# The router reads the residual through weights scaled by the modulation, and ACT modulates all channels there

## The chip, the cores and the metric

One core of one Trainium2 chip runs the whole program. The metric is device time in microseconds of one execution; the program before was executed three times for its median. TensorE (PE) multiplies, DVE and ACT work elementwise, SP issues the weight loads; POOL (GpSimd) does almost nothing.

## The reference, cut to what matters

Two layers (Hyena, then RG-LRU) are each followed by a mixture of 16 experts with a router that both share. 384 tokens (128 context, 256 latent) of width 1024 pass through. The part that the change touches is the norm, the modulation and the router before each expert layer:

```python
h = rms_norm(x, norm_moe[i]) * (1 + sc2) + sh2         # sc2, sh2 per stream: context or latent
scores = softmax(h @ router_w)                          # 16 experts
sel = scores + router_bias
best_group = argmax(sum of the top 2 of sel in each group of 4)
idx = top 2 of sel within best_group;  gates = scores[idx] / sum(scores[idx])
x = x + g2 * sum_j gates_j * ((silu(h @ w1[e_j]) * (h @ w3[e_j])) @ w2[e_j])
```

With r the reciprocal root of a token, h @ W = r * (x @ (norm_moe * (1 + sc2) * W)) + sh2 @ W. The program after the change computes the logits in this second form; h itself is still needed, by the experts.

## The kernel before, in words

Activations lie channel by channel: `xc` (the residual) and `hT` hold 8 channel tiles of 128 partitions by 384 tokens. Instructions of each engine are written out in order by hand, one function per engine (`_(sp)`, `_(act)`, `_(pe)`, `_(dve)`), and are tied by counting semaphores (`S("name")`); `before(name, index)` gives how many counts earlier layers or norms have made, from the table `PER`. A norm has a tag: 0 and 2 are those of the mixers, 1 and 3 those of the expert layers.

From the residual to the experts, for tags 1 and 3, the order is this. DVE adds each output tile to `xc` (L1760); ACT squares it (L559); TensorE sums the squares with a matrix of ones, in four column tiles of 32 (`norm_sums`); ACT takes the root (L571), DVE the reciprocal (L1440), TensorE spreads it over all partitions (`norm_spread`, products of `rs` with a column of the identity). DVE multiplies `xc` by it, channel by channel (L1447). Then `modulate` applies scale and shift: ACT to the first BY_ACT = 5 channels (two instructions each, one for each stream, L580), DVE to the last 3 (L1456). The router multiplies `rw` (16 experts padded to 32 columns) with `hT`: two accumulation steps in each of four column tiles, so that PSUM has four partial sums. ACT copies them (L810), TensorE transposes them, DVE adds the four parts (L1776), takes the maximum and subtracts it, ACT takes the exponential (L813) and DVE selects group and experts in some 27 small linked instructions up to the mask (L1819). TensorE counts with the mask each token's rank in its expert's queue; DVE makes one-hot matrices (`pick`, L1862) of the ranks. TensorE meanwhile transposes `hT` into token order, six tiles of four transposes (`token_tile`), which ACT evicts into `h` (L805). The first expert gathers its tokens as `h` times `pick` (the products PS<-stack,h).

`spin(n)` is n products whose result nobody reads. In `norm` one stands before and two behind the spread; in the router five stand behind the token tiles and three behind the ranks.

Every weight goes through ten slots of 2 MB, loaded by SP. At the residual's end four loads of the first two experts are released; the next waits for the route and the first expert's first product. A matmul of fp32 appears as two records in the trace.

Of the kernel before, what the change touches and what calls it, by code (L numbers as in the profile page):

```python
# [12 lines left out]
ALU = mybir.AluOpType  # L13
# [3 lines left out]
P = 128  # L17
D = 1024
KD = D // P
# [17 lines left out]
_COLS = [("ident", P), ("earlier_rows", P // 2), ("all_rows", P // 2), ("ones", 32), ("iota_base", BASE), ("iota_extra", EXTRA), ("limits", NX), ("desc", NE)]  # L37
# [36 lines left out]
def constants():  # L74
# [13 lines left out]
    put("iota_extra", np.tile(np.arange(EXTRA), (P, 1)))  # L88
    put("desc", np.tile(NE - np.arange(NE), (P, 1)))
# [35 lines left out]
class Chain:  # L125
# [5 lines left out]
    def link(self, instruction):  # L131
# [6 lines left out]
PER = dict(sq=8, ss_mm=1, rms=1, rinv=1, rb_mm=1, nrm=8, hT_act=BY_ACT, hT_dve=KD - BY_ACT, ada_mm=12, o_mm=8, x_upd=8,  # L138
           rt_mm=3, rt_ev=1, rt_exp=1, rt_max=1, rt_mask=1, tok_mm=6, tok=6, route=1, pick=18, gpick=16,
           xT_mm=16, xT=16, w1_mm=16, w13_mm=16, sig=16, hid=16, gpT_mm=8, gpT=8, hidT_mm=16, hidT=16, w2_mm=16, yo=16,  # L140
           c_mm=64, acc_done=64)
def before(name, index):

    return PER[name] * index

# [109 lines left out]
def program(nc, A, y_prompt, y_sample, new_state):  # L255
    where, (pool, pool_order, pool_count) = plan(), pool_plan()
    with ExitStack() as ctx:
# [91 lines left out]
        chosen = misc[:, 1728:1760].bitcast(BF16)  # L349
        earlier_rows, all_rows = const("earlier_rows").bitcast(BF16), const("all_rows").bitcast(BF16)  # L350
# [175 lines left out]
        def _(act):  # L526
# [46 lines left out]
            def modulate(tag):  # L573
# [3 lines left out]
                for k in range(BY_ACT):  # L577
# [10 lines left out]
            def norm(tag, sem, value):  # L588
# [4 lines left out]
                modulate(tag)  # L593
# [79 lines left out]
            def mixer0():  # L673
# [8 lines left out]
                modulate(0)  # L682
# [109 lines left out]
            for l in range(LAYERS):  # L792
# [9 lines left out]
                def token_tile(i):  # L802
                    act.wait_ge(S("tok_mm"), before("tok_mm", l) + i + 1)
# [3 lines left out]

                table(ACT.Exp)
                act.wait_ge(S("rt_mm"), before("rt_mm", l) + 1)
                a.activation(pre[:, 0, :], PS[:, 0, 0:N], ACT.Copy).then_inc(S("rt_ev"), 1)  # L810
                token_tile(0)
                act.wait_ge(S("rt_max"), before("rt_max", l) + 1)
                a.activation(rt(0), rt(0), ACT.Exp).then_inc(S("rt_exp"), 1)  # L813
                for i in range(1, 6):
                    token_tile(i)
# [28 lines left out]
        def _(pe):  # L844
# [136 lines left out]
            def channel_ready(tag, k):  # L981

                if k < BY_ACT:
                    pe.wait_ge(S("hT_act"), before("hT_act", tag) + k + 1)
                else:
                    pe.wait_ge(S("hT_dve"), before("hT_dve", tag) + k - BY_ACT + 1)

            def norm_ready(tag):
                pe.wait_ge(S("hT_act"), before("hT_act", tag + 1))
                pe.wait_ge(S("hT_dve"), before("hT_dve", tag + 1))  # L990

            def norm(tag):
                norm_sums(tag)
                if tag == 1:
                    pe.wait_ge(S("v_in"), 16)
                spin(1, bank=3)
# [1044 lines left out]
```

## Time and profile before

| | |
|---|---|
| three executions | 1561.53, 1564.23, 1564.71 us; median 1564.23 |
| the profiled execution | 1562.67 us, its span 1560.9 us |
| granted TensorE clock, mean | 0.993 |
| PE busy | 1499.3 us (96%) |
| DVE busy | 633.1 us (41%) |
| ACT busy | 297.5 us (19%) |
| DMA | 495.31 MB, mean 317 GB/s |

The span runs from the first to the last instruction; the execution's own time has the launch around it. Busy PE includes fillers, so 96% doesn't say that TensorE bounds all stages: what ends a stage is read from the chain of waits.

### The profile page before, as it was taken

The page shows a single profiled execution, that of the slowest core. Times are in us where ns is not written, and L with a number is a line of the kernel's source. Part 1 is how long each engine was busy: PE and PEld are TensorE (multiplying, and loading weights), DVE is VectorE, ACT ScalarE, POOL GpSimd, SP SyncE. Part 2 cuts the span into 40 slices and gives each one's busy share as a digit, 9 for nine tenths or more (in the row PEclk, how much of TensorE's full clock was granted, in tenths as well). Part 3 has the DMA queues.
Part 4 walks back from the last instruction along what each step waited for, and adds up shares of the span by engine and source line. Part 5 has one row for each costly group of instructions (what it writes and reads, how often), then busy time and mean ns, then how long its engine had stood idle before and what let it go on. Part 6 is the DMA issues. An engine that isn't in the chain of part 4 may idle for free.

```text
span 1560.9 us, 21439 instructions
## 1 busy us (share of the span) xinstructions
PE 1499.3 (96%) x7870; PEld 718.6 (46%) x7871; DVE 633.1 (41%) x1846; ACT 297.5 (19%) x503; POOL 0.2 (0%) x4
## 2 busy tenths in 40 slices
PE   9999999999899999999999899999999999999986
PEld 4454555654444344344353455555344434344433
DVE  4445665434324322322333548735132332432333
ACT  4422222121010011011010357623011001011001
POOL 0000000000000000000000000000000000000000
PEclk9999999999999999999999999999999999999999
DMA  9548667762969999999996701525899999999992
GB/s 345 186 138 304 252 253 266 290 278 113 418 278 396 426 427 427 426 426 427 427 423 240 254 1 54 215 109 216 365 423 425 427 426 422 425 427 426 425 393 95
DMA packets 67712, 495.31 MB, mean 317 GB/s; under 512 B 4608, under 2 KB 21264, under 8 KB 28368
## 3 DMA queue, kind: packets, MB, share of 16 engines
q1 hardware_dynamic: 66048, 489.33, 76.7%
q10 hardware_dynamic: 1616, 5.33, 1.0%
q8 instruction: 32, 0.52, 0.1%
q14 instruction: 16, 0.13, 0.0%
HBM read 493.06 MB, written 1.58 MB: 317 GB/s over the span
## 4 chain that ended last, share of the span: by engine, by line
PE 78%; DMA 11%; DVE 5%; ACT 3%; issue 1%; DVEq 0%; SPq 0%; ACTq 0%
PE PS L846 76%; DMA halves<-in_moe_w 11%; PE PS L850 2%; DVE xc L1872 1%; ACT hT L580 1%; DVE misc L1690 0%; DVE halves L1690 0%; DVE halves L1683 0%; DVE halves L1681 0%; ACT hT L829 0%; DVE halves L1509 0%; DVE halves L1682 0%; ACT halves L640 0%; ACT halves L742 0%; ACT h L641 0%
## 5 line engine op out<-in xcount | busy, mean ns | idle before, releaser
L846 PE MATMUL PS<-halves,hT 128*64 128x512 f32 x3072 | 670.1, 595 | 16.1 <-DMA halves<-in_moe_w 13.9
L846 PEld LDWEIGHTS PS<-halves,hT 128*64 128x64 f32 x3072 | 217.8, 137 | 450.1 <-issue 426.9
L846 PE MATMUL PS<-hT,halves 128*128 128x384 f32 x640 | 214.9, 490 | 0.1
L846 PE MATMUL PS<-halves 128*32 128x512 f32 (+5 forms) x928 | 194.1, 510 | 1.8 <-ACT halves L543 0.7
L846 PEld LDWEIGHTS PS<-hT,halves 128*128 128x128 f32 x640 | 119.3, 190 | 98.0 <-issue 18.2
L1953 DVE COPY misc<-PS 64x512 f32<-64x512 f32 x32 | 21.9, 683 | 320.9 <-PE PS L846 320.9
L846 PEld LDWEIGHTS PS<-halves 128*128 128x128 f32 (+2 forms) x928 | 96.6, 158 | 85.3 <-issue 44.4
L1872 DVE SCALAR_TENSOR_TENSOR xc<-PS,MOD,xc 128x128 f32<-128x128 f32 x336 | 112.4, 410 | 13.8 <-PE PS L846 11.8
L602 ACT ACTIVATE hT<-PS 128x512 f32<-128x512 f32 x32 | 19.1, 598 | 430.5 <-PE PS L846 430.5
L846 PE MATMUL PS<-stack,h 128*128 128x128 f32 x768 | 93.5, 279 | 5.4 <-issue 4.3
L846 PEld LDWEIGHTS PS<-stack,h 128*128 128x128 f32 x768 | 89.5, 194 | 18.1 <-issue 16.5
L1941 DVE TENSOR_TENSOR hT<-hT,PS 128x512 f32<-128x512 f32 x32 | 22.0, 688 | 152.1 <-PE PS L846 152.1
L617 ACT ACTIVATE hT<-PS 128x512 f32<-128x512 f32 x32 | 19.1, 597 | 310.8 <-PE PS L850 310.8
L1936 DVE TENSOR_TENSOR hT<-hT,PS 128x512 f32<-128x512 f32 x32 | 22.0, 687 | 103.4 <-ACT hT L602 103.4
L846 PE MATMUL PS<-hT,misc 128*128 128x384 f32 x128 | 53.1, 500 | 4.8 <-DVE RG L1953 3.3
L846 PE MATMUL PS<-hT,RG 128*128 128x384 f32 x128 | 51.3, 486 | 0.0
L1474 DVE SCALAR_TENSOR_TENSOR h<-pre,VT,h 128x127 f32<-128x127 f32 (+1 forms) x80 | 29.6, 412 | 43.9 <-ACT h L658 28.6
L654 ACT ACTIVATE pre<-PS,VT 128x384 f32<-128x384 f32 x24 | 14.0, 581 | 160.5 <-PE PS L846 160.5
L846 PE MATMUL PS<-h,halves 128*128 128x384 f32 x128 | 42.6, 486 | 0.0
L850 PE MATMUL PS<-cst,hT 128*128 128x128 f32 x224 | 35.0, 284 | 4.2 <-DVE xc L1872 3.3
L846 PE MATMUL PS<-halves,misc 128*32 128x256 f32 x640 | 35.6, 380 | 2.4 <-ACT misc L607 2.4
L850 PEld LDWEIGHTS PS<-cst,hT 128*128 128x128 f32 x224 | 30.5, 178 | 12.2 <-DVE xc L1872 4.4
(239 smaller groups left out, 1025.2 us busy)
## 6 DMA issues: line engine op xcount, KB each, us to landing
halves<-in_moe_w SPq DMA_DIRECT2D x192, 2048.0 KB, 17.8
halves<-in_ada_w SPq DMA_DIRECT2D x48, 1024.0 KB, 6.5
halves<-in_hy_w_in SPq DMA_DIRECT2D x12, 1024.0 KB, 5.2
halves<-in_rg_w_in SPq DMA_DIRECT2D x4, 2048.0 KB, 19.1
halves<-in_hy_w_out SPq DMA_DIRECT2D x4, 1024.0 KB, 9.4
halves<-in_rg_w_out SPq DMA_DIRECT2D x2, 2048.0 KB, 10.6
halves<-in_rg_wa SPq DMA_DIRECT2D x1, 2048.0 KB, 8.4
halves<-in_rg_wx SPq DMA_DIRECT2D x1, 2048.0 KB, 12.4
```

Source lines behind the costliest of these rows:

```text
L580: ins = a.activation(hT3[:, k, cs], hT3[:, k, cs], ACT.Identity, bias=MOD[:, l, 8 * sh + k, s:s + 1], scale=MODA[:, tag, k, s:s + 1])
L602: a.activation(hid, PS[:, 2, :], ACT.Sigmoid).then_inc(S("sig"), 1)
L617: a.activation(hidT, PS[:, 2, :].rearrange("p (c m) -> p c m", m=P), ACT.Copy) \
L654: a.activation(pre[:, ct % 2, :], PS[:, ct % 2, 0:N], ACT.Identity, bias=VT[:, 0, HB + ct:HB + ct + 1]).then_inc(S("in_ev0"), 1)
L846: return nc.tensor.matmul(out, lhsT, rhs, start=start, stop=stop)
L850: return nc.tensor.transpose(out, in_, ident[0:n, 0:n])
L1474: last = v.scalar_tensor_tensor(o, i, weight, o, ALU.mult, ALU.add)
L1872: ins = v.scalar_tensor_tensor(xc[:, k, cs], PS[:, bank, cs], MOD[:, l, 8 * G2 + k, s:s + 1], xc[:, k, cs], ALU.mult, ALU.add)
L1936: ch.link(v.tensor_tensor(hid, hid, PS[:, 2, :], ALU.mult))
L1941: v.tensor_tensor(hid, hid, PS[:, 3, :], ALU.mult).then_inc(S("hid"), 1)
L1953: last = v.tensor_copy(yo[g][BASE * r:BASE * r + BASE, :], PS[BASE * g:BASE * g + BASE, 6, :])
```

## The change

The names are those of the kernel. `by_act(tag)`, `turned_act` and `turned_dve` replace the fixed split: at odd tags all eight channels are ACT's. DVE scales the router's weights for both streams ahead of the residual's updates (`rw_mod`). TensorE multiplies the shift with the plain weights (two columns, one for each stream) and the residual with the scaled ones (`router_raw`), between the sums and the spread. ACT copies both results. DVE multiplies the copied logits by the reciprocal root, before it applies the norm to channels 0 to 5; `fold` is a constant of four stacked identities, with which TensorE adds the four partial sums, transposes, and adds the shift's part in one product pair per token tile. DVE takes maximum and difference from PSUM, then applies the norm to channels 6 and 7. ACT modulates channels 0 to 3, takes the exponential, modulates 4 to 7 and only then evicts the token tiles, in the order 0, 2, 4, 1, 3, 5. The fillers of the odd norms go; two stand behind the router's products, one behind the token tiles, three behind the ranks as before.

```diff
@@ -34,7 +34,7 @@
 NX = (N - BASE) // EXTRA
 
 
-_COLS = [("ident", P), ("earlier_rows", P // 2), ("all_rows", P // 2), ("ones", 32), ("iota_base", BASE), ("iota_extra", EXTRA), ("limits", NX), ("desc", NE)]
+_COLS = [("ident", P), ("earlier_rows", P // 2), ("all_rows", P // 2), ("ones", 32), ("iota_base", BASE), ("iota_extra", EXTRA), ("limits", NX), ("desc", NE), ("fold", NE)]
 _HYENA_COLS = [("fwd_lat", 2 * LAT), ("fwd_ctx", CTX), ("inv_lat", 4 * LAT // 2), ("inv_ctx", CTX)]
 COL, NCOL = {}, 0
 for _name, _n in _COLS + _HYENA_COLS:
@@ -86,6 +86,7 @@
     put("ones", np.ones((P, 32)))
     put("iota_base", np.tile(np.arange(BASE), (P, 1)))
     put("iota_extra", np.tile(np.arange(EXTRA), (P, 1)))
+    put("fold", np.tile(np.eye(32)[:, 0:NE], (4, 1)))
     put("desc", np.tile(NE - np.arange(NE), (P, 1)))
     put("limits", np.tile(BASE + EXTRA * np.arange(NX), (P, 1)))
     lag = []
@@ -135,13 +136,28 @@
 
 
 
-PER = dict(sq=8, ss_mm=1, rms=1, rinv=1, rb_mm=1, nrm=8, hT_act=BY_ACT, hT_dve=KD - BY_ACT, ada_mm=12, o_mm=8, x_upd=8,
-           rt_mm=3, rt_ev=1, rt_exp=1, rt_max=1, rt_mask=1, tok_mm=6, tok=6, route=1, pick=18, gpick=16,
+PER = dict(sq=8, ss_mm=1, rms=1, rinv=1, rb_mm=1, nrm=8, bias_mm=1, bias_ev=1, raw_mm=1, rw_mod=1, ada_mm=12, o_mm=8, x_upd=8,
+           rt_mm=2, rt_ev=1, rt_exp=1, rt_max=1, rt_mask=1, tok_mm=6, tok=6, route=1, pick=18, gpick=16,
            xT_mm=16, xT=16, w1_mm=16, w13_mm=16, sig=16, hid=16, gpT_mm=8, gpT=8, hidT_mm=16, hidT=16, w2_mm=16, yo=16,
            c_mm=64, acc_done=64)
 def before(name, index):
 
     return PER[name] * index
+
+
+def by_act(tag):
+
+    return KD if tag % 2 else BY_ACT
+
+
+def turned_act(tag):
+
+    return sum(by_act(u) for u in range(tag))
+
+
+def turned_dve(tag):
+
+    return KD * tag - turned_act(tag)
 
 
 
@@ -570,11 +588,11 @@
                 act.wait_ge(S("ss_mm"), tag + 1)
                 a.activation(rs, PS[:, NORM_BANK[tag], 0:96], ACT.Sqrt, bias=eps, scale=1.0 / D).then_inc(S("rms"), 1)
 
-            def modulate(tag):
+            def modulate(tag, ks):
                 l = tag // 2
                 sh = SH2 if tag % 2 else SH1
                 act.wait_ge(S("modA"), tag + 1)
-                for k in range(BY_ACT):
+                for k in ks:
                     act.wait_ge(S("nrm"), before("nrm", tag) + k + 1)
                     for s, cs in streams:
                         ins = a.activation(hT3[:, k, cs], hT3[:, k, cs], ACT.Identity,
@@ -590,7 +608,8 @@
                     table(ACT.Sqrt)
                 squares(tag, NORM_ORDER[tag], sem, value)
                 norm_root(tag)
-                modulate(tag)
+                if tag % 2 == 0:
+                    modulate(tag, range(BY_ACT))
 
             def expert_layer(l):
                 with act.Fori(0, NE // UNROLL) as group:
@@ -799,20 +818,24 @@
 
                 norm(2 * l + 1, "x_upd", 8 * l + 1)
 
-                def token_tile(i):
-                    act.wait_ge(S("tok_mm"), before("tok_mm", l) + i + 1)
+                def token_tile(n):
+                    i = TOKEN_ORDER[n]
+                    act.wait_ge(S("tok_mm"), before("tok_mm", l) + n + 1)
 
                     a.activation(h[:, i // 2, i % 2 * HALF:i % 2 * HALF + HALF].rearrange("p (k c) -> p k c", k=4),
                                  PS[:, 2 + i, :].rearrange("p (c k) -> p k c", k=4), ACT.Copy).then_inc(S("tok"), 1)
 
+                act.wait_ge(S("bias_mm"), l + 1)
+                a.activation(bias_col, PS[:, 4, 0:2], ACT.Copy).then_inc(S("bias_ev"), 1)
+                act.wait_ge(S("raw_mm"), l + 1)
+                a.activation(pre[:, 0, :], PS[:, 5, 0:N], ACT.Copy).then_inc(S("raw_ev"), 1)
                 table(ACT.Exp)
-                act.wait_ge(S("rt_mm"), before("rt_mm", l) + 1)
-                a.activation(pre[:, 0, :], PS[:, 0, 0:N], ACT.Copy).then_inc(S("rt_ev"), 1)
-                token_tile(0)
+                modulate(2 * l + 1, range(4))
                 act.wait_ge(S("rt_max"), before("rt_max", l) + 1)
                 a.activation(rt(0), rt(0), ACT.Exp).then_inc(S("rt_exp"), 1)
-                for i in range(1, 6):
-                    token_tile(i)
+                modulate(2 * l + 1, range(4, KD))
+                for n in range(6):
+                    token_tile(n)
                 for i, bank in enumerate(TOKEN_BANKS):
                     act.wait_ge(S("xT_mm"), before("xT_mm", l) + i + 1)
                     a.activation(xT[:, i, :, :], PS[:, bank, :].rearrange("p (c m) -> p c m", m=P), ACT.Copy) \
@@ -981,21 +1004,23 @@
             def channel_ready(tag, k):
 
                 if k < BY_ACT:
-                    pe.wait_ge(S("hT_act"), before("hT_act", tag) + k + 1)
+                    pe.wait_ge(S("hT_act"), turned_act(tag) + k + 1)
                 else:
-                    pe.wait_ge(S("hT_dve"), before("hT_dve", tag) + k - BY_ACT + 1)
+                    pe.wait_ge(S("hT_dve"), turned_dve(tag) + k - BY_ACT + 1)
 
             def norm_ready(tag):
-                pe.wait_ge(S("hT_act"), before("hT_act", tag + 1))
-                pe.wait_ge(S("hT_dve"), before("hT_dve", tag + 1))
+                pe.wait_ge(S("hT_act"), turned_act(tag + 1))
+                pe.wait_ge(S("hT_dve"), turned_dve(tag + 1))
 
             def norm(tag):
                 norm_sums(tag)
-                if tag == 1:
-                    pe.wait_ge(S("v_in"), 16)
-                spin(1, bank=3)
-                norm_spread(tag)
-                spin(2, bank=3)
+                if tag % 2:
+                    router_raw(tag // 2)
+                    norm_spread(tag)
+                else:
+                    spin(1, bank=3)
+                    norm_spread(tag)
+                    spin(2, bank=3)
 
             def in_tile(ct):
                 w = piece(("in", ct // 2)).rearrange("p (k n) -> p k n", k=8)
@@ -1141,22 +1166,39 @@
                     last = tr(PS[:, 2 + i, P * c:P * c + P], hT3[:, 4 * half + c, P * t:P * t + P])
                 last.then_inc(S("tok_mm"), 1)
 
-            def router(l):
-                pe.wait_ge(S("rw_in"), 16)
+            def router_raw(l):
+                pe.wait_ge(S("rw_mod"), l + 1)
                 for kk in range(2):
                     for j in range(4):
-                        channel_ready(2 * l + 1, j + 4 * kk)
-                        last = mm(PS[32 * j:32 * j + 32, 0, 0:N], rw[:, j + 4 * kk, :], hT3[:, j + 4 * kk, :],
+                        last = mm(PS[32 * j:32 * j + 32, 4, 0:2], rw[:, j + 4 * kk, :], MOD[:, l, 8 * SH2 + j + 4 * kk, :],
                                   kk == 0, kk == 1)
-                last.then_inc(S("rt_mm"), 1)
-                token_tile(l, 0)
+                last.then_inc(S("bias_mm"), 1)
+                for s, cs in streams:
+                    for kk in range(2):
+                        for j in range(4):
+                            last = mm(PS[32 * j:32 * j + 32, 5, cs], rw_mod[:, s, j + 4 * kk, :], xc[:, j + 4 * kk, cs],
+                                      kk == 0, kk == 1)
+                last.then_inc(S("raw_mm"), 1)
+
+            def router(l):
+                pe.wait_ge(S("bias_ev"), l + 1)
                 pe.wait_ge(S("rt_ev"), before("rt_ev", l) + 1)
                 for t in range(NT):
-                    last = tr(PS[:, 1, P * t:P * t + P], pre[:, 0, P * t:P * t + P])
+                    s = 0 if t == 0 else 1
+                    out = PS[:, 6, NE * t:NE * t + NE]
+                    mm(out, bias_col[:, s:s + 1].broadcast_to([P, P]), const("fold"), True, False)
+                    last = mm(out, pre[:, 0, P * t:P * t + P], const("fold"), False, True)
                 last.then_inc(S("rt_mm"), 1)
-                for i in range(1, 6):
+                if l == 0:
+                    pe.wait_ge(S("v_in"), 16)
+                spin(2)
+                for n, i in enumerate(TOKEN_ORDER):
+                    if n in (0, 3):
+                        pe.wait_ge(S("hT_act"), turned_act(2 * l + 1) + 4 * (i % 2) + 4)
+                    if 2 + i == 6:
+                        pe.wait_ge(S("rt_max"), before("rt_max", l) + 1)
                     token_tile(l, i)
-                spin(5)
+                spin(1)
                 pe.wait_ge(S("rt_mask"), before("rt_mask", l) + 1)
                 mask = e3(chosen[:, 0:3 * NE])
                 mm(PS[:, 1, 0:4 * NE], earlier_rows, chosen, True, False)
@@ -1439,16 +1481,15 @@
                 dve.wait_ge(S("rms"), tag + 1)
                 v.reciprocal(rs, rs).then_inc(S("rinv"), 1)
 
-            def norm_apply(tag):
+            def norm_apply(tag, ks):
                 if tag % 2 == 0 and tag:
                     dve.wait_ge(S("acc_done"), ADDED + before("acc_done", tag // 2))
                 dve.wait_ge(S("rb_mm"), tag + 1)
-                for k in range(KD):
+                for k in ks:
                     v.tensor_tensor(hT3[:, k, :], xc[:, k, :], PS[:, 1, 0:N], ALU.mult).then_inc(S("nrm"), 1)
 
             def modulate(tag):
-                l = tag // 2
-                sh = SH2 if tag % 2 else SH1
+                l, sh = tag // 2, SH1
                 dve.wait_ge(S("modA"), tag + 1)
                 for k in range(BY_ACT, KD):
                     dve.wait_ge(S("nrm"), before("nrm", tag) + k + 1)
@@ -1754,6 +1795,12 @@
                     for s, cs in streams:
                         ins = v.tensor_scalar(xc[:, dc, cs], xc[:, dc, cs], gb[:, dc, s:s + 1], None, ALU.add)
                 link(ins)
+                dve.wait_ge(S("modA"), 2 * l + 2)
+                dve.wait_ge(S("rw_in"), 16)
+                for s in range(2):
+                    ins = v.tensor_tensor(rw_mod[:, s, :, :], rw[:, :, :],
+                                          MODA[:, 2 * l + 1, :, s:s + 1].broadcast_to([P, KD, 32]), ALU.mult)
+                ins.then_inc(S("rw_mod"), 1)
                 for dc in range(KD):
                     dve.wait_ge(S("o_mm"), 8 * l + dc + 1)
                     for s, cs in streams:
@@ -1770,12 +1817,18 @@
                 def wide(ap, n=NE):
                     return ap.unsqueeze(2).broadcast_to([P, NT, n])
 
-                link(v.memset(chosen[:, 3 * NE:], 0.0))
-                dve.wait_ge(S("rt_mm"), before("rt_mm", l) + 2)
-                parts = PS[:, 1, 0:N].rearrange("p (t j e) -> p t e j", t=NT, j=4)[:, :, 0:NE, :]
-                link(v.tensor_reduce(L, parts, AX, ALU.add))
-                link(v.tensor_reduce(mx, L, AX, ALU.max))
-                v.tensor_tensor(L, L, wide(mx), ALU.subtract).then_inc(S("rt_max"), 1)
+                tag = 2 * l + 1
+                v.memset(chosen[:, 3 * NE:], 0.0)
+                norm_inverse(tag)
+                dve.wait_ge(S("raw_ev"), l + 1)
+                dve.wait_ge(S("rb_mm"), tag + 1)
+                v.tensor_tensor(pre[:, 0, :], pre[:, 0, :], PS[:, 1, 0:N], ALU.mult).then_inc(S("rt_ev"), 1)
+                norm_apply(tag, range(6))
+                dve.wait_ge(S("rt_mm"), before("rt_mm", l) + 1)
+                logits = PS[:, 6, 0:NT * NE].rearrange("p (t e) -> p t e", t=NT)
+                link(v.tensor_reduce(mx, logits, AX, ALU.max))
+                v.tensor_tensor(L, logits, wide(mx), ALU.subtract).then_inc(S("rt_max"), 1)
+                norm_apply(tag, range(6, KD))
                 dve.wait_ge(S("rt_exp"), before("rt_exp", l) + 1)
                 link(v.tensor_reduce(sm, L, AX, ALU.add))
                 link(v.reciprocal(sm, sm))
@@ -1826,7 +1879,7 @@
                 link(v.tensor_reduce(sm, scores, AX, ALU.add))
                 link(v.reciprocal(sm, sm))
                 link(v.tensor_tensor(gates[:, :, 0:NE], scores, wide(sm), ALU.mult))
-                dve.wait_ge(S("rt_mm"), before("rt_mm", l) + 3)
+                dve.wait_ge(S("rt_mm"), before("rt_mm", l) + 2)
                 ranks = PS[:, 1, 0:NT * NE].rearrange("p (t e) -> p t e", t=NT)
                 link(v.scalar_tensor_tensor(eq, ranks, 1.0, mask, ALU.add, ALU.mult))
                 link(v.tensor_scalar(rankm[:, :, 0:NE], eq, -1.0, None, ALU.add))
@@ -1962,7 +2015,6 @@
                     norm(2 * l)
                     mixer1()
                 residual(l)
-                norm(2 * l + 1)
                 route(l)
                 expert_layer(l)
 
@@ -1990,6 +2042,7 @@
 SPREAD_BANKS = (6, 4, 5, 7, 1, 0, 3, 4)
 
 TOKEN_BANKS = (0, 5)
+TOKEN_ORDER = (0, 2, 4, 1, 3, 5)
 X_COMBINE = ((0, 0), (2, 2), (4, 6), (6, 4), (1, 5), (3, 7), (5, 3), (7, 1))
 
 _INS = ["ada_w", "norm_final", "hy_w_in", "hy_f_w3", "hy_w_out", "rg_w_in", "rg_wa", "rg_wx", "rg_w_out", "moe_w1",
```

## Rows read from the trace of the kernel before

**Rows 1.** page part 4, the chain's shares by engine

```profile
PE 78%; DMA 11%; DVE 5%; ACT 3%; issue 1%; DVEq 0%; SPq 0%; ACTq 0%
```

**Rows 2.** chain of waits in order of time, layer 0: start, us, what

```profile
342.57 1.15 PE PS L846 x8
...
344.39 4.49 ACT hT L580 x10
348.89 1.28 ACT L586
350.82 0.56 PE PS L850 x3
361.24 1.08 DVE stack L1862 x6
...
621.42 23.30 DMA halves<-in_moe_w
```

**Rows 3.** timeline of DVE, layer 0: start, us, instruction, count, idle

```profile
321.53 0.74 DVE L1760 SCALAR_TENSOR_TENSOR xc<-PS,MOD,xc 128x128 f32<-128x128 f32 x2 [15.68 <-PE PS L846]
...
343.74 3.81 DVE L1447 TENSOR_TENSOR hT<-xc,PS 128x384 f32<-128x384 f32 x8 [1.22 <-PE PS L846]
...
352.98 0.20 DVE L1780 TENSOR_REDUCE misc<-misc 128x3 f32<-128x48 f32 x1 [0.31 <-ACT misc L813]
...
358.87 0.21 DVE L1819 TENSOR_TENSOR misc<-misc 128x48 bf16<-128x48 f32 x1
...
360.41 0.21 DVE L1831 SCALAR_TENSOR_TENSOR misc<-PS,misc 128x48 f32<-128x48 f32 x1
```

**Rows 4.** timeline of ACT, layer 0

```profile
350.19 0.20 ACT L586 ACTIVATE small<-small 128x1 f32<-128x1 f32 x1
...
352.70 0.24 ACT L813 ACTIVATE misc<-misc 128x48 f32<-128x48 f32 x1 [1.31 <-DVE misc L1778]
352.85 2.53 ACT L805 ACTIVATE h<-PS 128x512 f32<-128x512 f32 x5
```

**Rows 5.** timeline of TensorE, layer 0

```profile
351.21 2.35 PE L850 MATMUL PS<-cst,hT 128*128 128x128 f32 x20
353.39 4.46 PE L846 MATMUL PS<-VT,cst 128*128 128x512 f32 x10
359.14 0.26 PE L846 MATMUL PS<-misc,cst 128*128 128x64 bf16 x4 [1.29 <-DVE misc L1819]
```

**Rows 6.** busy us by window: PE, PEld, DVE, ACT, POOL; clock, DMA share, GB/s

```profile
362.00:384.00 22.00, 21.08 (x138) 10.82 (x137) 6.97 (x33) 3.07 (x4) 0.00 (x0) 1.00 0.00 1
```

**Rows 7.** chain of waits, layer 1

```profile
1063.99 1.15 PE PS L846 x8
...
1065.81 4.49 ACT hT L580 x10
```

**Rows 8.** timeline of DVE, layer 1

```profile
1045.47 0.74 DVE L1760 SCALAR_TENSOR_TENSOR xc<-PS,MOD,xc 128x128 f32<-128x128 f32 x2 [3.44 <-PE PS L846]
...
1074.04 0.20 DVE L1780 TENSOR_REDUCE misc<-misc 128x3 f32<-128x48 f32 x1 [0.31 <-ACT misc L813]
```

**Rows 9.** timeline of TensorE, 14 to 42 us

```profile
32.13 2.79 PE L846 MATMUL PS<-cst,halves 128*128 128x32 f32 x24
```

**Rows 10.** timeline of TensorE, 340.7 to 344 us

```profile
340.51 0.74 PE L846 MATMUL PS<-h,cst 128*32 128x96 f32 x12
```

**Rows 11.** groups by form, 318 to 420 us: busy, mean ns | idle before

```profile
L846 PE MATMUL PS<-halves,misc 128*32 128x256 f32 x128 | 7.1, 380 | 0.5 <-ACT misc L607 0.5
...
L846 PE MATMUL PS<-h,cst 128*32 128x96 f32 x64 | 1.7, 249 | 0.1
...
L1896 DVE TENSOR_TENSOR misc<-misc,PS 128x256 f32<-128x256 f32 x1 | 0.4, 422 | 2.6 <-PE PS L846 2.6
```

**Rows 12.** busy time by window, layer 1, with the granted clock

```profile
1100.00:1106.00 6.00, 3.55 (x16) 1.04 (x13) 0.69 (x1) 0.00 (x0) 0.00 (x0) 1.00 1.01 429
1107.00:1113.00 6.00, 5.12 (x14) 1.86 (x14) 0.00 (x0) 0.60 (x1) 0.00 (x0) 0.50 0.99 418
```

More of the change, by code:

```diff
@@ L349, in program @@
         chosen = misc[:, 1728:1760].bitcast(BF16)
+        bias_col = misc[:, 1792:1794]
+        rw_mod = misc[:, 2304:2304 + 2 * KD * 32].rearrange("p (s k e) -> p s k e", s=2, k=KD)
         earlier_rows, all_rows = const("earlier_rows").bitcast(BF16), const("all_rows").bitcast(BF16)
@@ L681, in mixer0 @@
                 spectrum(1)
-                modulate(0)
+                modulate(0, range(BY_ACT))
                 for ct in range(24):
@@ L1461, in norm @@
                 norm_inverse(tag)
-                norm_apply(tag)
+                norm_apply(tag, range(KD))
                 modulate(tag)
@@ L1576, in mixer0 @@
                 halves_joined(0)
-                norm_apply(0)
+                norm_apply(0, range(KD))
                 filter_norm(0)
```

## The prediction

> **What bounds the kernel now.** I read the page's chain shares first: TensorE is on the chain for 78% of the span, DMA for 11%, DVE 5%, ACT 3% [rows 1]. So an edit beside TensorE's products counts only where TensorE waits. The chain in order of time shows two such places that the diff touches, one per layer: from the end of the residual to the first gather. There it leaves TensorE for ACT's modulation, returns to the router's products, and ends in DVE's one-hot picks at 361.24 [rows 2]. The timelines of DVE, ACT and TensorE in that stretch then say which wait ends last. The reader is to see that DVE's top-2 selection, from its first sum of the exponentials (352.98) to the mask (358.87 + 0.21 = 359.08), is one unbroken chain of 6.10 us [rows 3], and that what feeds it is late by a series of steps: spread of the root (ends 342.57 + 1.15 = 343.72), five channels of modulation on ACT (4.49), eight router products, a copy, three transposes, reductions, exponential [rows 2, 3, 4]. Meanwhile TensorE runs fillers: 10 records in 4.46 us between the transposed tokens and the mask [rows 5].
>
> Does time won there reach the end? DMA streams weights in the expert layers and bounds some of them (23.30 us in one piece at 621.42, [rows 2]), but it stands still from 362 to 384, share 0.00 [rows 6]: all slots are full and the next load waits for the first expert's product, which waits for the route. Both streams therefore start earlier by what the route is earlier. I pass the gain on whole.
>
> **The change, step by step.** I call S the end of the spread.
>
> Before, DVE's first sum starts at S + 9.26 in layer 0 (352.98 - 343.72) and at S + 8.90 in layer 1 (1074.04 - 1065.14) [rows 2, 3, 7, 8].
>
> After, from S: DVE scales the raw logits (one instruction) and then applies the norm; eight such take 3.81, so 0.476 each. ACT began 0.65 after DVE's first (344.39 - 343.74), so it now begins at S + 0.02 + 0.476 + 0.65 = S + 1.15. It modulates four channels, 8 instructions of the 10 that took 4.49, 3.59: S + 4.74. Then the exponential; DVE started its sum 0.28 after ACT started that (352.98 - 352.70) [rows 2, 3, 4]: S + 5.02. DVE's side of this: seven instructions to S + 3.35, a maximum and a subtraction of about 0.25 each (0.21 and some 0.03 between them), S + 3.85, then norm channels 6 and 7, S + 4.80. So ACT ends last, by 0.2. Gain from S: 4.24 and 3.88.
>
> TensorE's router (two small products per token tile, 12 records) must be done by S + 3.35. It starts at S + 0.6. Records with 128x128 weights and few columns: 24 took 2.79, 0.116 each [rows 9], so 1.4 and S + 2.0. If they took the 0.144 of the spread's eight (1.15) it would be S + 2.3: hidden either way, with 1 us to spare.
>
> S itself moves. Before, the last sums end at 340.51 + 0.74 = 341.25 and the spread starts at 342.57, when DVE's reciprocal is there; a filler covers the gap [rows 2, 10]. Now 16 records of 2 columns, 16 of 128 and 16 of 256 columns stand there. No row shows 2 or 128 columns with 32-column weights; 96 columns took 1.7/64 = 0.027 each and 256 took 7.1/128 = 0.056 [rows 11]. I take 0.025, 0.030 and 0.056: 0.4 + 0.5 + 0.9 = 1.8, end 343.05, and the spread's 1.15 behind it: S = 344.2, later by 0.45 (0.5 in round figures; the same in layer 1). Lower bound 0: the products disappear in the wait. Upper bound: all 48 at 0.056, 2.7 us, S later by 1.35.
>
> Net: 4.24 - 0.45 = 3.8 and 3.88 - 0.45 = 3.4, together 7.2 us.
>
> What is hidden: the scaled weights cost DVE two products of 128x256; one such from PSUM took 0.42 [rows 11], so 0.85 per layer (bounds 0.4, two of the 128x48 kind, and 1.1, two of 128x384). In layer 0 they fall into DVE's idle 15.68 us before the first residual update, in layer 1 into the 3.44 before the fifth [rows 3, 8]; without that cover they would cost their 0.85. ACT's copy of the bias column lies beside the reciprocal (its size is between nothing and the 0.47 of a 128x384); the raw copy of about 0.5 ends near 343.6 and lies beside the spread. The exp table load (1.28, [rows 2]) moves from behind the modulation to in front of it: 343.6 + 1.5 = 345.1, while modulation can start at 345.35: hidden by 0.2. Table rule: ACT's next instruction started at 350.19, 1.30 after the load began at 348.89 [rows 2, 4].
> The Trainium skill (ScalarE: Activation LUTs, "What ACT_TABLE_LOAD costs") adds a drain of about 1.4 us to every switch and counts about 2.7 in all. This trace does not show a drain here, so I use the row; by the page modulation would start some 1.1 us later in each layer, an estimate, and the run would end near 1559.2.
>
> The selection after the sum is unchanged: mask at S + 11.12, picks 3.2 later. Who could be late for it now? ACT modulates the other four channels until S + 5.0 + 3.6 = S + 8.6, then evicts six token tiles at 0.506 (five took 2.53, [rows 4]): S + 11.65, while the gather comes at S + 14.35. 2.7 us to spare. On TensorE the second three token tiles wait for S + 8.6 and take 1.4 (20 transposes 2.35, [rows 5]), one filler 0.9: S + 10.9, just before the mask's S + 11.12. The rank products (0.26) have another 1.3 us until DVE reads them (360.41, [rows 3, 5]). Waiting instructions on TensorE hold only token tiles and fillers behind them. SP's queue and its loads are untouched and are released by the same counts; POOL has no part.
>
> **Sum.** The profiled execution took 1562.67 (span 1560.9 and 1.8 around it). 1562.67 - 7.2 = 1555.5. The runs' median, 1564.23, stands 1.56 above that execution, so I forecast 1564.2 - 7.2 = 1557.0.
>
> **The rivals.**
> First, products in front of the spread at the dear end. For it: nothing shows their size. Against: at 96 columns a record already takes 0.027. Each layer then keeps 2.9 and 2.5, together 5.4: 1558.8.
>
> Second, the clock. From 1100 to 1106 TensorE was busy 3.55 of 6 us and still at level 1.00 (2.4 GHz); the stretch 1107 to 1113, behind an idle 2.45 us, has 0.50 (1.2 GHz) [rows 12]. The change makes such a hole: nothing for TensorE between the first three token tiles (S + 6.2) and the other three (S + 8.6), 2.4 us, and less dense work before it. If the level falls there, the three tiles take 2.8 and the filler 1.8: TensorE is free at S + 13.2, ranks at S + 13.7 instead of the needed S + 12.4, 1.3 us lost per layer: 1564.2 - 7.2 + 2.6 = 1559.6. Against: two fillers stand right before S + 4.8, and in a fall around S + 2 they are what is slowed, at no cost. I give it a fifth; one layer alone is as likely as both, so it reaches down to 1558.3.
> The Trainium skill (TensorE: Matmul & The Clock Gate, "Part 4: PE-mode transpose") says that transposes do not count as busy for the clock gate. If so, the time from S + 4 to S + 10 holds no counted work at all and the fall would be the rule in both layers. In this trace the level was 1.00 through the present transposes, but dense fillers follow them at once [rows 5], so it settles nothing; the price is the 1559.6 above.
>
> Third, slower than before: TensorE stays at 1.2 GHz after the mask into work that bounds the kernel, the gather and the first expert's products. Every microsecond of that work done at full level costs one more, so 3.6 us of gain are used up once 7.2 us of the path run at 1.2 GHz. The longest stretch at 0.50 that I found amid the kernel is the 6 us of [rows 12], a little more at its ends, and only part of it was path. At 10 us per layer the loss is 5 against 3.6, twice: 1567. Against it: three fillers (2.7 us) still stand between ranks and gather.
>
> Fourth, the change doesn't shorten what it says: DVE, not ACT, is last because the router's products reach it after S + 3.35. They would have to take 0.28 per record, as 128-column ones with nothing overlapped, then 3.4 us: DVE waits until S + 4.0, channels 6 and 7 end at S + 5.5, 0.5 lost per layer: 1558.0. It lies in the forecast's own range.
>
> **Chances.** Forecast with its own range 1555 to 1558.5 (the fourth inside): 0.55. First 0.15, second 0.18, the table rule 0.03, slower 0.04. What is left, 0.05, is pauses of TensorE with no releaser (2.45 us, [rows 12]) that fall elsewhere in longer code, either way. A measurement of this kernel can tell 0.2%, 3.1 us, from no change. Faster by more: below 1561.1, all but the third, part of the pauses and a clock that falls more often than said: 0.84. Within: 0.11. Slower: 0.05. Range 1554.0 (S unmoved, 8.1 us, and the lowest of the runs shown instead of their median) to 1561.4.
>
> **What would show it.** Spread starts near 343.1 rather than 342.57; ACT modulates 8 + 8 instructions with the exponential between, DVE's sum at S + 5.0; TensorE idle 2.4 us before the fourth token tile; DVE's picks end 3.8 and 3.4 us earlier in the two layers; first expert product earlier by the same. Wrong if the sum starts later than S + 6, if S moves by over 1.4, if the clock is below 1.00 between router and first expert in both layers, or if weights arrive late in the first two experts.

## The result and the profile after

The changed kernel takes 1636.02 us (median of 4 executions, 1633.83 to 1646.4) against 1564.20 us: ratio 1.047, interval 1.0447 to 1.0492. It is 72 us slower; I had forecast 7 faster.

The router did what was forecast. The chain of waits of the changed kernel, layer 0 (start, us, what), answers to [rows 2]:

```profile
338.04 0.76 DVE xc L1807 x2
...
339.40 2.88 PE PS L869 x61
...
343.48 3.61 ACT hT L598 x8
...
355.51 1.08 DVE stack L1915 x6
356.73 20.97 PE PS L869 x136
```

From the last residual update to the first gather it is 18.69 us (338.04 to 356.73), where the kernel before had 22.93 (339.52 to 362.45): 4.24 less. Layer 1 has 18.70 (1136.02 to 1154.72) in place of 22.57: 3.87 less. The loss lies behind it. Below are the page's shares by engine, its instruction queue (packets, MB, share) and three groups of TensorE's products; a group's columns are busy us, mean ns, and idle us before with what ended it:

```profile
PE 82%; issue 6%; DVE 5%; DMA 5%; ACT 3%; ACTq 0%; DVEq 0%; SPq 0%
```

```profile
q8 instruction: 96, 1.57, 0.4%
```

```profile
L869 PE MATMUL PS<-halves,hT 128*64 128x512 f32 x3072 | 683.4, 604 | 55.1 <-issue 48.2
...
L869 PE MATMUL PS<-stack,h 128*128 128x128 f32 x768 | 98.5, 289 | 16.2 <-issue 15.1
...
L869 PE MATMUL PS<-hT,misc 128*128 128x384 f32 x128 | 54.1, 509 | 15.1 <-issue 10.3
```

"issue" has 6% of the chain, before 1% [rows 1]; it is time for which the trace names nobody who is waited for. In the kernel before these groups had 16.1 us idle (DMA 13.9), 5.4 (issue 4.3) and 4.8 (DVE 3.3), and queue q8, that of instructions, 32 packets and 0.52 MB. So TensorE waits 48.2 + (15.1 - 4.3) + 10.3 = 69 us more on nobody, and 64 more packets of instructions are brought in. TensorE's timeline shows where (start, us, instruction, count, idle before):

```profile
425.95 0.49 PE L873 MATMUL PS<-cst,hT 128*128 128x128 f32 x3
426.37 7.09 PE L869 MATMUL PS<-halves,hT 128*64 128x512 f32 x32
441.17 5.08 PE L869 MATMUL PS<-halves,hT 128*64 128x512 f32 x12 [7.71 <-issue]
```

The loop body holds two experts and is run eight times, with seven jumps back. The 32 records are the last product (w2) of the body's second expert, the 12 are the first (w1) of the next turn: the pause is the jump back. All seven jumps back in layer 0 have one, 6.5 to 7.7 us, 48.2 in all; in layer 1 none has. A second kind, 1.8 to 2.4 us, stands where the body jumps forward over the unused extra pass: eleven of them in layer 0, 23.0 us in all. The kernel before has this kind only in the first turn of each layer. The clock pays as well: 1.00 before this pause, 0.50 in the middle of it and still 0.50 for the products behind it.

```profile
426.00:433.00 7.00, 7.00 (x36) 2.41 (x34) 0.00 (x0) 2.26 (x3) 0.00 (x0) 1.00 1.00 421
...
436.00:440.00 4.00, 0.00 (x0) 0.00 (x0) 2.15 (x13) 0.00 (x0) 0.00 (x0) 0.50 1.01 418
...
441.00:444.00 3.00, 2.83 (x8) 0.98 (x10) 0.00 (x0) 0.00 (x0) 0.00 (x0) 0.50 0.96 396
```

(The three rows are from separate answers of one view, busy time by window.) The three groups are busy for 683.4 + 98.5 + 54.1 = 836.0 us instead of 670.1 + 93.5 + 53.1 = 816.7: 19 us for products at 1.2 GHz. From first gather to the next norm's reciprocal layer 0 takes 608.3 us, before 527.5: 80.8, which is 69 + 19 less some 8. Of the 8 most are waits for weights that the pauses now cover: DMA ended 13.9 us of idle time in the first group before, at most 6.9 after. With 8.1 won at the two routers and 1.5 before the first one, the span is 71 longer.

### The profile page after: what moved, and what is told of

It reads as the page before. It is cut to its first block, busy times and chain, and to the rows that moved or that the text cites. A ratio compares the mean times of both kernels' runs of the same rounds, so it can differ in the third digit from the quotient of the medians.

```text
span 1632.0 us, 21567 instructions
## 1 busy us (share of the span) xinstructions
PE 1506.1 (92%) x7932; PEld 726.5 (45%) x7933; DVE 631.4 (39%) x1838; ACT 302.4 (19%) x517; POOL 0.2 (0%) x4
## 4 chain that ended last, share of the span: by engine, by line
PE 82%; issue 6%; DVE 5%; DMA 5%; ACT 3%; ACTq 0%; DVEq 0%; SPq 0%
PE PS L869 80%; DMA halves<-in_moe_w 5%; PE PS L873 2%; DVE xc L1925 1%; ACT hT L598 1%; DVE misc L1731 0%; DVE halves L1731 0%; DVE halves L1724 0%; DVE halves L1722 0%; ACT hT L852 0%; DVE halves L1550 0%; DVE halves L1723 0%; ACT halves L659 0%; ACT halves L761 0%; ACT h L660 0%
## 5 line engine op out<-in xcount | busy, mean ns | idle before, releaser
L869 PE MATMUL PS<-halves,hT 128*64 128x512 f32 x3072 | 683.4, 604 | 55.1 <-issue 48.2
L869 PE MATMUL PS<-stack,h 128*128 128x128 f32 x768 | 98.5, 289 | 16.2 <-issue 15.1
L869 PEld LDWEIGHTS PS<-stack,h 128*128 128x128 f32 x768 | 94.2, 203 | 29.2 <-issue 27.6
L869 PE MATMUL PS<-hT,misc 128*128 128x384 f32 x128 | 54.1, 509 | 15.1 <-issue 10.3
L673 ACT ACTIVATE pre<-PS,VT 128x384 f32<-128x384 f32 x24 | 13.9, 580 | 160.5 <-PE PS L869 160.5
L869 PEld LDWEIGHTS PS<-hT,misc 128*128 128x128 f32 x128 | 22.3, 193 | 37.9 <-issue 21.8
```

The costliest lines, as they stand in the source:

```text
L673: a.activation(pre[:, ct % 2, :], PS[:, ct % 2, 0:N], ACT.Identity, bias=VT[:, 0, HB + ct:HB + ct + 1]).then_inc(S("in_ev0"), 1)
L869: return nc.tensor.matmul(out, lhsT, rhs, start=start, stop=stop)
```

## The experiments

Theory 1: the place of the expert loop in TensorE's instruction stream decides. The loop body is 1580 instructions by count of the built program (a product of fp32 is four, a transpose two); the new router puts 62 more ahead of layer 0's loop and 124 ahead of layer 1's. (The pages agree: products and weight loads together are 124 more, 7932 + 7933 for 7870 + 7871.) Theory 2: the new router (order, memory, clock) slows the loop. Theory 3: more instructions as such.

The tool is N instructions that do nothing, ahead of both loops (waits on a semaphore long satisfied; the build joins two to one instruction), in `a_` kernels on the changed kernel, in `b_` kernels on the one before. Each kernel has its own number in place of 2 * N:

```diff
             def mixer0():
                 spin(4, RG)
+                for _ in range(2 * N):
+                    pe.wait_ge(S("spin_rows"), 1)
```

All of them, with the place of each loop's first instruction and, in brackets, what is left of it modulo 256, the block size that the Trainium skill gives (Runtime: NRT & Kernel Launch, "Instruction fetch mechanics"). "One" marks the time of a single execution. The last column is layer 0's time from the first gather to the next norm's reciprocal, the 527.5 us of above.

| kernel | loop 0 at | loop 1 at | us | ratio to before | layer 0's loop, us |
|---|---|---|---|---|---|
| before | 3451 (123) | 6639 (239) | 1564.2 | | 527.5 |
| after | 3513 (185) | 6763 (107) | 1636.0 | 1.047 | 608.3 |
| b_pad62 | 3513 (185) | 6701 (45) | 1653.8 | 1.056 [1.048, 1.064] | 617.7 |
| b_pad128 | 3579 (251) | 6767 (111) | 1571.6 | 1.004 [1.002, 1.006] | 529.4 |
| a_pad128 | 3641 (57) | 6891 (235) | 1568.4 | 1.0025 [1.0007, 1.0042] | 530.8 |
| a_pad64 | 3577 (249) | 6827 (171) | 1563.7, one | | 530.0 |
| a_pad48 | 3561 (233) | 6811 (155) | 1555.5 | 0.9945 [0.9926, 0.9964] | 528.1 |
| a_less32 | 3481 (153) | 6731 (75) | 1560.2 | 0.997 [0.996, 0.999] | 529.1 |
| a_short | 3513 (185) | 6699 (43) | 1553.8 | 0.992 [0.990, 0.995] | 527.0 |
| b_mid216 | 3451 (123) | 6855 (199) | 1682.3, one | | 529.3 |
| a_pad22 | 3535 (207) | 6785 (129) | 1558.1, one | | 528.0 |
| a_pad36 | 3549 (221) | 6799 (143) | 1559.9, one | | 529.3 |
| b_pad46 | 3497 (169) | 6685 (29) | 1636.2, one | | 595.3 |
| b_pad36 | 3487 (159) | 6675 (19) | 1569.1, one | | 528.9 |

**Place against router.** N = 62 in the kernel before, N = 128 and 64 in the changed one, N = 128 in the one before as control.

> The kernel before with 62 such satisfied waits on TensorE ahead of the first layer's expert loop, the number by which the change moves that loop. Theory 1: the loop of layer 0 stands where it stands in the changed kernel and pauses the same way; 1564 + 72 + the 8 us that only the new router wins = about 1644, at least 1630. Theory 2: 1564 to 1568, no pause at the turns.

> The changed kernel with 128 more instructions on TensorE, all waits on a semaphore that is long satisfied, ahead of the first layer's expert loop; nothing else. Theory 1 (place in the instruction stream): in the changed kernel TensorE stands still for 6.5 to 7.7 us at each turn of the first layer's expert loop and for about 2 us at each skipped extra pass, because the loop, 62 instructions later than before, lies badly against the blocks in which instructions are brought in. Moved by another 128 it lies well again in both layers: no pauses, the router's gain of 4.2 + 3.9 us stays, 1555 to 1558 us. The Trainium skill (Runtime: NRT & Kernel Launch, 'Instruction fetch mechanics') speaks of blocks of 256 instructions; half a block is the estimate behind the 128. Theory 2 (the new router itself, its order or its memory, slows the loop): the pauses stay, 1634 to 1640 us.

> The kernel before with 128 such waits, the control of a_pad128: is a kernel with more instructions slower or faster by itself? Theory 1: the loop lies well in both layers, 1562 to 1567 us, no pause at the turns. Theory 3 (every added instruction costs, or the whole program's length decides): pauses as in b_pad62 or more, over 1630.

> The changed kernel with 64 such waits. Theory 1: layer 0's loop is free of pauses, since 64 further instructions bring it out of the bad stretch, which is 44 of 256 places wide if bad means that the loop of 1580 instructions lies in one block more than it must (an estimate from the 256 of the Trainium skill, Runtime: NRT & Kernel Launch, 'Instruction fetch mechanics'). Layer 1's loop comes near that stretch: 1555 to 1559 us if it misses it, about 1630 if it meets it. Theory 2: 1634 to 1640 us with the pauses in layer 0.

The kernel before, with its old router, becomes the slow one by 62 instructions that do nothing: 80 and 99 us in its two executions, median 90, with pauses at all seven jumps back (b_pad62, TensorE's timeline, below). The old router has the pauses where the place is the same, and the new one loses them where it is another: theory 2 falls. With 128 the pauses at the jumps back are gone in both, so theory 3 falls too.

```profile
439.58 6.18 PE L846 MATMUL PS<-halves,hT 128*64 128x512 f32 x28
453.64 11.73 PE L846 MATMUL PS<-halves,hT 128*64 128x512 f32 x42 [7.88 <-issue]
```

The forecast 1555 to 1558 for a_pad128 was a miss, and b_pad128's 1562 to 1567 as well: so many waits cost time where they stand, and I had put them at nothing. TensorE's timeline of a_pad128 has them as one idle stretch near the start:

```profile
18.12 1.61 PE L869 MATMUL PS<-hT 64*128 64x384 f32 x2 [8.80 <-issue]
```

Its first gather comes 12.9 us later than the changed kernel's (369.66 and 356.73), so 8.8 of that is traced and the rest isn't. In b_pad128 the stretch is 6.75.

a_pad64 met neither of its two forecasts, 1555 to 1559 or about 1630. Layer 1's loop, at 171, pauses at one of its seven jumps back, 4.28 us, and the next turn's two forward jumps have 1.9 and 2.2 (page and timeline):

```profile
q8 instruction: 42, 0.69, 0.2%
...
1324.14 6.21 PE L869 MATMUL PS<-halves,hT 128*64 128x512 f32 x20 [4.28 <-issue]
```

This gives the price of a paused jump back, with the forward jumps of its turn, in packets of instructions. a_pad64 has 42 of them where a_pad48 and a_pad22, without such a pause, have 33: nine for one jump. b_pad62 and b_pad46, with seven paused jumps each, have 95 where the kernel before and b_pad36 have 32: 63, again nine a jump. So in a paused turn instructions are brought in again. DMA is fully busy with weights in that time (share 1.01 from 436 to 440); whether a pause would be shorter without them no run shows.

**A cure with few or no waits.** N = 48, and in a_less32 eight fillers fewer, 32 instructions, and no wait:

```diff
-                spin(4, RG)
+                spin(1, RG)
                 pe.wait_ge(S("f_sin"), 1)
                 mm(PS[:, 1, 0:N], f_w2, f_h1, True, True).then_inc(S("f_mm"), 1)
-                spin(5, RG)
```

> The changed kernel with 48 satisfied waits on TensorE ahead of layer 0's loop. The runs so far: both kernels are slow where that loop starts at instruction 3513 of the stream (by count of the built program) and not at 3451, 3577, 3579 or 3641, and layer 1's loop paused a little at 6827 and not at 6639, 6763 or 6891. Theory 1: at 3561 and 6811 both lie well; 1554 to 1558 us, that is faster than the kernel before by 6 to 8. If layer 0's loop still pauses, the bad stretch reaches further than 48 places and the time is about 1630.

> The changed kernel with 8 fillers fewer at its start (spin(4) becomes spin(1), spin(5) goes), which are 32 instructions: nothing is added, and layer 0's loop starts at 3481, layer 1's at 6731. Theory 1: no pauses at the turns, 1554 to 1560 us; the fillers gone may leave TensorE at 1.2 GHz for some of the first products, 0 to 4 us. A theory by which only added instructions were a cure, or the waits themselves, expects 1634 as in the changed kernel.

The pauses are gone in both. a_pad48 is as expected; a_less32, at 1560.2, is at the upper end of its 1554 to 1560. a_pad48 is the version that beats both kernels: 8.7 us (0.5%) less than the one before, an interval clear of 1, and 80 less than the changed one. Its page and, for the place that had paused for 7.71 us, its timeline:

```profile
q8 instruction: 33, 0.54, 0.1%
...
L869 PE MATMUL PS<-halves,hT 128*64 128x512 f32 x3072 | 669.7, 594 | 19.1 <-DMA halves<-in_moe_w 16.8
```

```profile
426.50 0.49 PE L873 MATMUL PS<-cst,hT 128*128 128x128 f32 x3
426.92 9.66 PE L869 MATMUL PS<-halves,hT 128*64 128x512 f32 x44
```

The 44 records are w2 and the next w1 without a gap between them, and DMA again ends most of TensorE's idle time. That a_less32, which only takes instructions away, is cured as well shows that the waits are no remedy by themselves.

**Place or length.** The same start as in the changed kernel, a shorter body (tokens of two of three tiles are left out of the extra passes' gather, so the result of those passes is incomplete):

```diff
-                    gather(l, 0, 4, Xpick, width).then_inc(S("x_G_mm"), 1)
+                    for g in range(4):
+                        last = mm(PS[32 * g:32 * g + 32, 0, 0:width], Xpick[:, 0, :],
+                                  h[:, 0, width * g:width * g + width], True, True)
+                    last.then_inc(S("x_G_mm"), 1)
```

> The changed kernel with a shorter loop at the same place: the gather of the extra pass takes one of three token tiles (4 products instead of 12, in both experts of the body), so tokens of the other two tiles are left out of the extra passes. Layer 0's loop starts at 3513 as in the changed kernel but is 1516 instructions long instead of 1580. Theory 1 in its sharper form, that the loop pauses when it touches one block more than TensorE can keep (by the 256 and 2048 instructions of the Trainium skill, Runtime: NRT & Kernel Launch, 'Instruction fetch mechanics', a start 212 or more places into a block is bad at 1580, and none is at 1536 or less; an estimate): no pauses, 1548 to 1556 us. If the start alone decides: pauses, about 1625.

No pause at any jump back; its page and its timeline at the same place:

```profile
q8 instruction: 32, 0.52, 0.1%
```

```profile
431.39 0.49 PE L873 MATMUL PS<-cst,hT 128*128 128x128 f32 x3
431.81 13.53 PE L869 MATMUL PS<-halves,hT 128*64 128x512 f32 x62
```

So the start alone doesn't decide; the length takes part. The loop's end moved here too, by 64 places. That the place of the end alone decides would fit as well, since in all other kernels start and end move together.

**The other layer, and blocks of 256.** 216 instructions in the second mixer of the kernel before, between the loops:

```diff
             for i in range(12, 16):
                 in_tile1(i)
+            for _ in range(432):
+                pe.wait_ge(S("spin_rows"), 1)
             for q in range(2):
                 ready(("out", 1, q))
```

> The kernel before with 216 satisfied waits on TensorE in the second mixer, between the two expert loops: layer 0's loop stays at 3451, layer 1's goes from 6639 to 6855. Theory 1 with blocks of 256 (the figure of the same page): 6855 is 3342 behind 3513, 14 places past a multiple of 256, so layer 1's loop should now pause at each turn as layer 0's did: 70 to 95 us more, and 10 to 20 us for the waits, 1640 to 1680 in all. If the bad place is one of layer 0 alone: 1575 to 1590.

Layer 0 is free, and layer 1, free in the kernel before and in the changed one, pauses at each of its seven jumps back, with 96 packets again. From gather to end it takes 576 us instead of 477. The waits cost 17.8 us here, and together the time, 1682.3, is a little above the 1680 forecast. A place in layer 1 that is bad lies 3342 behind one in layer 0 that is. 256 fits as the period (13 times and 14 over), but the free and bad starts of this table allow others too, 277 or 333 for instance; 128 they exclude. What speaks for 256 beside them is the size of a packet: 0.52 MB in 32 is 16.3 KB, and the Trainium skill (the page named above the table, same section) gives a block of 256 instructions 16 KiB.

```profile
1160.33 7.09 PE L846 MATMUL PS<-halves,hT 128*64 128x512 f32 x32
1175.45 4.76 PE L846 MATMUL PS<-halves,hT 128*64 128x512 f32 x12 [8.04 <-issue]
```

**The edges.**

> One of two looks for the far edge of the bad stretch: the changed kernel with 22 satisfied waits ahead, layer 0's loop at 3535, layer 1's at 6785. In steps of 256 the paused starts so far are at 185 (3513) and 199 (6855), a half-paused one at 171 (6827), and the free ones at 123, 153, 233, 249, 251 and 57. If the stretch is as wide as the sharper form of theory 1 says (44 places, an estimate from the Trainium skill, Runtime: NRT & Kernel Launch, 'Instruction fetch mechanics'), it runs from about 170 to 214, and 3535, at 207, pauses at each turn: 1625 to 1650 us. If a stretch only as wide as 171 to 200 is bad: 1554 to 1560.

> The other look: 36 satisfied waits, layer 0's loop at 3549 (221 in its block of 256), layer 1's at 6799. Sharper form of theory 1: past the edge at 214, no pauses, 1552 to 1560 us. If the stretch reaches up to the free 233: 1625 to 1650.

> The near edge, on the kernel before: 46 satisfied waits put layer 0's loop at 3497, 169 in its block of 256. The start at 207 turned out free, so the bad stretch ends between 199 and 207. If it is 44 places wide it begins between 156 and 163, and this loop pauses at each turn: 1630 to 1660 us. If it is narrower than 37 places, this loop is free: 1563 to 1570 us.

> 36 waits, layer 0's loop at 3487, 159 in its block. By a width of 44 this lies at the very edge, 156 to 163, and may go either way; narrower than 40: free, 1563 to 1570 us; paused (1630 to 1660 us) only if the stretch is 41 or more places wide.

a_pad22 went against the expectation, a_pad36 with it: 207 is free. b_pad46 then pauses and b_pad36 doesn't. In b_pad46, just inside, the first jump back has a pause of 4.07 us and a second one of 1.09 follows a few records later; the other six have 2.3 to 3.3 and 0.3 to 1.9:

```profile
446.38 2.67 PE L846 MATMUL PS<-halves,hT 128*64 128x512 f32 x8 [4.07 <-issue]
450.15 5.25 PE L846 MATMUL PS<-halves,hT 128*64 128x512 f32 x14 [1.09 <-issue]
```

The bad starts are 169, 185 and 199, the free ones 153, 159, 207 and beyond; 171, in layer 1, paused at one jump of seven. If both layers share one stretch, it is at least 31 and at most 47 places wide. The Trainium skill (same page and section) gives TensorE room for 2048 instructions, eight blocks of 256, refilled by block, and says that a taken branch whose target isn't in the current window of blocks stalls for the fetch. By it 1580 instructions touch eight blocks, all there are, from some 44 of 256 starts and seven from the others, and a body up to 1536 never eight; an estimate, with which the width and a_short agree. Why a body that touches all eight should be too much, the estimate doesn't say.

Two things don't come out. Counted from the block's border the bad starts would be 213 to 255 by this estimate, and 221, 233, 249 and 251 are free: the true stream would have to be 49 to 53 instructions ahead of my count, which no run shows. And 171 in layer 1 would have to be as bad as 169 and 185 in layer 0, which it isn't.

That instructions are fetched again in the paused turns is shown by the packets; that the loop's place brings it on, by b_pad62 and a_less32; that its length takes part, by a_short. That eight blocks touched is the condition is supported and not shown. The page calls TensorE's hold 2048 and in the same section speaks of a window of two blocks for engines in general: with two, every jump back in every kernel here would stall, and they don't.

## Why the prediction was wrong

Point by point, by its own steps.

- **The chain from S on** was right. DVE's first sum starts at 347.26; S is 339.40 + 2.88 = 342.28, the end of TensorE's piece of the chain, so S + 4.98, forecast S + 5.02. The timelines of ACT and DVE show the order that was worked out, ACT last by a little:

```profile
343.48 3.61 ACT L598 ACTIVATE hT<-hT,MOD,MODA 128x128 f32<-128x128 f32 x8 [0.21 <-DVE hT L1489]
347.00 0.23 ACT L835 ACTIVATE misc<-misc 128x48 f32<-128x48 f32 x1
```

```profile
345.99 1.01 DVE L1489 TENSOR_TENSOR hT<-xc,PS 128x384 f32<-128x384 f32 x2
347.26 0.20 DVE L1833 TENSOR_REDUCE misc<-misc 128x3 f32<-128x48 f32 x1 [0.26 <-ACT misc L835]
```

- **The move of S** was put at 0.45 and is nearly nothing: from the last update's start to S it is 4.24 us after and 4.20 before (339.52 to 343.72). The lower bound was the truth. The 16 records of 2 columns take 0.28 and the 32 others 1.49, nearly all of it under the wait for DVE's reciprocal, which ends at 340.97:

```profile
339.59 0.28 PE L869 MATMUL PS<-MOD,rw 128*32 128x2 f32 x16
339.71 1.49 PE L869 MATMUL PS<-xc,misc 128*32 128x128 f32 x32
341.13 1.13 PE L869 MATMUL PS<-rs,cst 128*128 128x96 f32 x8
...
347.15 1.53 PE L873 MATMUL PS<-cst,hT 128*128 128x128 f32 x12 [0.79 <-ACT hT L598]
350.79 1.53 PE L873 MATMUL PS<-cst,hT 128*128 128x128 f32 x12 [2.11 <-ACT hT L598]
```

  So the routers gave 8.1 us, not 7.2. The first and fourth rivals are out.
- **The scaled weights** took DVE 0.76 us in layer 0 (forecast 0.85), in idle time ahead of the first update, as forecast.
- **The table load** took 1.28 us and the next instruction started 1.30 after it (341.77, 343.07), no drain, as in [rows 2, 4].
- **The hole in TensorE's work** before the fourth token tile is there, 2.11 us. The clock stayed at 1.00 through layer 0's router in the changed kernel and was 0.76 on average from 1142 to 1149 in layer 1's. In a_pad48 it was at 0.51 from 344 to 351, under the two fillers and the token tiles, and yet its residual-to-gather time is the same, 18.69 us (338.21 to 356.90): the second rival's fall happens, at no cost. That the transposes alone bring it about isn't shown.

```profile
344.00:351.00 7.00, 7.00 (x23) 4.77 (x23) 6.15 (x26) 7.00 (x18) 0.00 (x0) 0.51 0.99 420
```

- **"I pass the gain on whole"** is the step that failed. I asked of the expert loops only whether weights arrive in time, and so put at nothing what the added instructions themselves do to the loops behind them. The trace before has three pauses of 2.0 to 2.5 us in the loops:

```profile
426.02 4.22 PE L846 MATMUL PS<-stack,h 128*128 128x128 f32 x24 [2.35 <-issue]
...
1105.44 2.57 PE L846 MATMUL PS<-VT,cst 128*128 128x512 f32 x4 [2.45 <-issue]
...
1134.39 2.94 PE L846 MATMUL PS<-stack,h 128*128 128x128 f32 x24 [1.98 <-issue]
```

  I filed them under "pauses of TensorE with no releaser", 0.05 of chance and one such pause in size. They stand where the first turn jumps forward over the extra pass, and every kernel here has them, a_pad48 too (2.48, 2.29, 2.42): they are no part of the loss, but they are the same pauses at a jump whose target had not been executed before, and so a sign that I could have read. In fact 62 instructions more are what moves a loop of 1580 instructions into the stretch where it is fetched again at each turn, 80.8 us in layer 0.
- **What the gain itself was worth**, a_pad48 shows: 1555.5 against the forecast 1557.0. From the first gather on its layer 0 takes 528.1 us, the kernel before 527.5. Where the loop lies well, the gain is passed on whole, as argued.
- **Slower** had 0.05, 0.04 of it on the clock. The clock did cost 19 us, but as a consequence of the pauses.

## What to carry to other kernels

Before an edit that adds or removes instructions ahead of a hardware loop, count the instructions of the loop's body on that engine. Here a body of 1580 was slow from some starts and fast from others, and one of 1516 was fast from a start that was slow for 1580. At such sizes the loop's place is a parameter of its own, and a change is judged fairly only after a few shifts of it. The sign in a profile is idle time with "issue" as releaser at the same point of each turn and more packets in the instruction queue; the proof is the old kernel with as many idle instructions as the change adds.

## What the runs showed of the hardware that was not expected

- Either layer's loop can be the slow one: layer 0's from 185, layer 1's from 199. The near edge is soft: 2.3 to 4.1 us a jump and a second pause of 0.3 to 1.9 from 169, against 6.1 to 7.9 from 185.
- A turn with a paused jump brings in nine packets of instructions more, of 16.3 KB each.
- A satisfied wait is not free on TensorE: 216 of them (432 calls) kept it idle for 17.8 us, 0.08 each. In a_pad128 the idle stretch is 8.8 us for 128 of them, 0.07 each.
- Sixteen fp32 records of 2 columns in four column tiles take 0.28 us in all, where I had taken 0.4.
